# Side work of a transformer block rescheduled: weighting ahead of the feed on VectorE, evacuation ahead of the exponentials on ScalarE

## The reference, cut to what matters

```python
# block 1: mixer with two attentions, then experts
h = rms_norm(x); z = h @ w_in                   # 2848 columns and two gates of 1024
out_a = fox_attention(norm(q), norm(k), v, log_sigmoid(f + b_forget)) @ w_fox_up   # 8 heads of 64
out_b = nsa_attention(...) @ w_nsa_up           # 8 heads: window, selected and compressed keys
x = x + (sigmoid(g_a) * out_a + sigmoid(g_b) * out_b) @ w_out
x = x + moe(rms_norm(x))                        # 16 experts, 4 groups, top-2 within the top-1 group
# compressed keys and values: gelu(blocks @ w1) @ w2, once for keys and once for values
# layers 0 and 1, each
z = rms_norm(x) @ w_in_2                        # q f i z of a gated recurrence; q k v z of an attention
att = silu(za) * softmax(rope(q) rope(k) + band, with sinks) v        # 16 heads of 64, window 128
hg = recurrence(silu(q), bounded sigmoid(f), i), normed and times silu(z)
x = x + rms_norm([hg, att] @ w_out_2)
```

## Time and profile before

| | |
|---|---|
| time, median of 3 runs | 1223.36 us (1220.58 to 1223.96) |
| the profiled execution's own time | 1213.91 us |
| its span, first to last instruction | 1212.1 us |
| mean granted clock of PE | 0.945 |
| busy: PE, DVE, ACT, POOL | 1063.1, 851.1, 663.9, 44.8 us |
| memory read | 209 MB, 173 GB/s over the span |

### The profile page before, as it was taken

The page is one execution under the profiler, slowest core; times in us unless marked ns, Lnnn a source line. Parts: engine busy times, 40 slices in busy tenths (PEclk is TensorE's granted clock), DMA queues, the critical chain, the costliest instruction groups (busy, mean ns, idle before and its releaser), DMA issues.

```text
span 1212.1 us, 16479 instructions
## 1 busy us (share of the span) xinstructions
PE 1063.1 (88%) x6109; PEld 908.8 (75%) x6109; DVE 851.1 (70%) x1653; ACT 663.9 (55%) x1318; POOL 44.8 (4%) x44
## 2 busy tenths in 40 slices
PE   5798888797799999999978798799988879779997
PEld 4675866687688787878858787688777868668876
DVE  5657744574599999999857565586656755658673
ACT  5334534554588888788743657422444365642342
POOL 0201000000101000010000000000100000000010
PEclk9989989898799999999989988899999889889999
DMA  8412316133199999999933323223335322223320
GB/s 329 174 70 81 129 38 236 75 111 134 54 395 366 365 373 357 376 357 386 355 122 132 112 105 105 70 105 132 129 139 191 136 77 102 105 70 131 113 104 35
DMA packets 30035, 211.31 MB, mean 174 GB/s; under 512 B 3584, under 2 KB 3712, under 8 KB 4992
## 3 DMA queue, kind: packets, MB, share of 16 engines
q1 hardware_dynamic: 28368, 205.01, 45.5%
q10 hardware_dynamic: 1584, 5.20, 1.2%
HBM read 209.15 MB, written 1.05 MB: 173 GB/s over the span
## 4 chain that ended last, share of the span: by engine, by line
PE 48%; DVE 29%; ACT 11%; DMA 7%; issue 3%; POOL 1%; SPq 0%; DVEq 0%; POOLq 0%; ACTq 0%
PE ps L505 12%; DVE w_lo L396 11%; PE ps L507 11%; PE ps L506 11%; DMA ring<-in_panels 7%; PE ps L510 4%; PE ps L940 3%; ACT s_buf L1798 3%; ACT w_hi L1751 3%; PE ps L655 2%; DVE s_buf L399 2%; DVE s_buf L396 2%; DVE stat L1197 1%; PE ps L711 1%; DVE scr L396 1%
## 5 line engine op out<-in xcount | busy, mean ns | idle before, releaser
L396 DVE TENSOR_TENSOR w_lo<-ring,w_hi 128x512 fp32r<-128x512 f32 x760 | 482.3, 689 | 180.0 <-ACT w_hi L1751 178.9
L1751 ACT ACTIVATE w_hi<-ring 128x512 fp32r<-128x512 f32 x760 | 426.0, 620 | 206.1 <-PE ps L507 165.5
L505 PE MATMUL ps<-w_hi,op_hi 128*128 128x512 f32 (+2 forms) x800 | 317.6, 397 | 19.8 <-ACT zin L1751 4.9
L507 PE MATMUL ps<-w_hi,op_lo 128*128 128x512 f32 (+2 forms) x800 | 310.3, 388 | 0.0
L506 PE MATMUL ps<-w_lo,op_hi 128*128 128x512 f32 (+2 forms) x800 | 310.2, 388 | 0.0
L505 PEld LDWEIGHTS ps<-w_hi,op_hi 128*128 128x128 f32 x800 | 152.5, 191 | 55.2 <-DVE w_lo L396 11.9
L507 PEld LDWEIGHTS ps<-w_hi,op_lo 128*128 128x128 f32 x800 | 152.5, 191 | 31.0
L506 PEld LDWEIGHTS ps<-w_lo,op_hi 128*128 128x128 f32 x800 | 152.7, 191 | 27.3
L505 PE MATMUL ps<-op_hi,w_hi 128*128 128x256 f32 x544 | 161.1, 296 | 1.2 <-DVE op_lo L396 1.2
L506 PE MATMUL ps<-op_lo,w_hi 128*128 128x256 f32 x544 | 157.0, 289 | 0.0
L507 PE MATMUL ps<-op_hi,w_lo 128*128 128x256 f32 x544 | 156.5, 288 | 0.0
(11 more groups left out here) (245 smaller groups left out, 1135.2 us busy)
## 6 DMA issues: line engine op xcount, KB each, us to landing
ring<-in_panels SPq DMA_DIRECT2D x194, 1024.0 KB, 6.5
cst<-in_c ACTq DMA_DIRECT2D x1, 1219.0 KB, 5.3
buf_a<-in_pre ACTq DMA_DIRECT2D x2, 512.0 KB, 6.7
keys<-in_post ACTq DMA_DIRECT2D x2, 512.0 KB, 3.4
out<-x_tok SPq DMA_DIRECT2D x2, 512.0 KB, 2.6
cst<-in_c ACTq DMA_DIRECT2D x1, 960.0 KB, 6.3
x_tok<-in_x SPq DMA_DIRECT2D x1, 512.0 KB, 4.7
x_tok<-in_x ACTq DMA_DIRECT2D x1, 512.0 KB, 4.9
```

Source lines behind the costliest of these rows:

```text
L396: return V.tensor_tensor(o, a, b, op)
L505: T.matmul(o, l[0], r[0], start=start, stop=False)
L507: return T.matmul(o, l[1], r[0], start=False, stop=stop)
L1751: return A.activation(o, a, ACT.Copy, scale=scale)
```

## The change

It moves side work between takes and changes the order within a take. On DVE `ahead` runs weigh and scores_out first and the feed after them. On ACT the exponentials move from `ahead` to `behind`, so a take's evacuation stands between the copy of transposes and the exponentials. In block 1 the head sums and norms are one step each for q and k, the forget gate's inputs come at take 11, its products behind the k transposes, `lower` (bounds and router split) at take 4, nsa_gates at 12, gate_on at 39 behind the compress step. Both products of the compress MLP go into one bank side by side, with one Gelu behind the second. In the layers rope and its transposes are three steps each (q half, q half, k); the last four attention rows come one take earlier; za_on is two halves at 13 and 20; qf_on is at 29 and 33 (26 and 34 before), att_split at 37 and 39 (34 and 35 before).

```diff
@@ -85,7 +85,7 @@
-SWA_AT = (13, 15, 17, 19, 22, 24, 27, 29, 31, 33)
+SWA_AT = (13, 15, 17, 19, 22, 24, 26, 28, 30, 32)
...
@@ -153,28 +153,30 @@
 def beside_block1():
-    table = {9: [("fox_sums", 0)], 11: [("fox_norms", 0)], 12: [("fox_q", 0)], 13: [("fox_k", 0)],
-             20: [("win_sums", 0)], 21: [("win_norms", 0), ("nsa_gates", 0), ("nsa_side", 0)], 22: [("nsa_side", 1)],
-             23: [("nsa_side", 2)], 24: [("slc_sums", 0)], 25: [("slc_norms", 0)], 26: [("nsa_side", 3)],
-             38: [("gate_on", 0)], 41: [("gate_on", 1)]}
+    table = {4: [("lower", 0)], 9: [("fox_sums", 0)], 10: [("fox_sums", 1)], 11: [("fox_norms", 0), ("forget", 0)],
+             12: [("fox_norms", 1), ("fox_q", 0), ("nsa_gates", 0)], 13: [("fox_k", 0)],
+             20: [("win_sums", 0)], 21: [("win_norms", 0), ("nsa_side", 0)], 22: [("nsa_side", 1)],
+             23: [("nsa_side", 2)], 24: [("slc_sums", 0)], 25: [("slc_norms", 0)], 26: [("nsa_side", 3)]}
-    table.setdefault(43, []).append(("up_split", 0))
+    for take, name, arg in ((39, "gate_on", 0), (41, "gate_on", 1), (43, "up_split", 0)):
+        table.setdefault(take, []).append((name, arg))
 def beside_layer(l):
-    table = {b + 9: [("rope", l)], b + 11: [("swa_sides", l)]}
+    table = {b + take: [(name, (l, i))] for take, name, i in (
+        (4, "rope", 0), (6, "swa_sides", 0), (8, "rope", 1), (9, "rope", 2), (10, "swa_sides", 1), (11, "swa_sides", 2))}
-    for take, name, arg in ((18, "za_on", l), (26, "qf_on", (l, 0)), (27, "qf_bound", (l, 0)), (34, "qf_on", (l, 1)),
-                            (34, "att_split", (l, 0)), (35, "qf_bound", (l, 1)), (35, "att_split", (l, 1))):
-        table.setdefault(b + take, []).append((name, arg))
+    for take, name, i in ((13, "za_on", 0), (20, "za_on", 1), (29, "qf_on", 0), (30, "qf_bound", 0), (33, "qf_on", 1),
+                          (34, "qf_bound", 1), (37, "att_split", 0), (39, "att_split", 1)):
+        table.setdefault(b + take, []).append((name, (l, i)))
...
@@ -600,17 +602,17 @@
                 pe.wait_ge(heads_done, 1)
                 for i in range(2):
                     pair_turns(ZFQ + 2 * i * P, 2 + i, z3).then_inc(side_T, 1)
+
+            def fox_k_(_):
+                pe.wait_ge(heads_done, 2)
+                for i in range(2):
+                    pair_turns(ZFK + 2 * i * P, 4 + i, z3).then_inc(side_T, 1)
                 pe.wait_ge(ld_c1, 16)
                 pe.wait_ge(forget, 1)
                 lf2 = stat[:, 64:80]
                 T.matmul(ps[:, 6, 0:8], ntri[:, 0:P], lf2[:, 0:8], start=True, stop=True)
                 T.matmul(ps[:, 6, 8:16], ntri[:, P:2 * P], lf2[:, 0:8], start=True, stop=False)
                 T.matmul(ps[:, 6, 8:16], ntri[:, 0:P], lf2[:, 8:16], start=False, stop=True).then_inc(side_T, 1)
-
-            def fox_k_(_):
-                pe.wait_ge(heads_done, 2)
-                for i in range(2):
-                    pair_turns(ZFK + 2 * i * P, 4 + i, z3).then_inc(side_T, 1)
 
             def nsa_side(n):
                 c, kind = SIDES[n]
...
@@ -701,17 +703,15 @@
-                    if step == 4:
-                        pe.wait_ge(cmp_a, 1)
-                            m = T.matmul(ps[0:64, 7, 0:256], blk[c][:, 8 * h + n, :, :].rearrange("p g n -> p (g n)"),
+                            m = T.matmul(ps[0:64, 7, c * 256:(c + 1) * 256], blk[c][:, 8 * h + n, :, :].rearrange("p g n -> p (g n)"),
-                    pe.wait_ge(cmp_a, 2)
+                    pe.wait_ge(cmp_a, 1)
...
@@ -1093,10 +1095,10 @@
-            def fox_sums(_):
+            def fox_sums(n):
-                head_sums(HEADS_FOX)
+                head_sums(HEADS_FOX[n:n + 1])
             def win_sums(_):
...
@@ -1118,21 +1120,26 @@
+            def fox_q(_):
+                lf, lx, la = stat[:, 64:80], stat[:, 80:96], stat[:, 96:112]
+                dve.wait_ge(forget_l, 1)
+                dv(ts(lx, lx, 0.0, None, ALU.min))
+                settle()
+                tt(lf, lx, la, ALU.subtract).then_inc(forget, 1)
-                dve.wait_ge(forget_l, 1)
-                dv(ts(lx, lx, 0.0, None, ALU.min))
-                settle()
-                tt(lf, lx, la, ALU.subtract).then_inc(forget, 1)
-                dve.wait_ge(side_T, 3)
-                ts(stat[:, 112:128], ps[:, 6, 0:16], -1.0, None, ALU.mult).then_inc(side, 1)
             def fox_k_(_):
-                    dve.wait_ge(side_T, 4 + i)
+                    dve.wait_ge(side_T, 3 + i)
+                dve.wait_ge(side_T, 5)
+                ts(stat[:, 112:128], ps[:, 6, 0:16], -1.0, None, ALU.mult).then_inc(side, 1)
+            def lower(_):
...
@@ -1249,7 +1256,7 @@
-                dve.wait_ge(za_on, l + 1)
+                dve.wait_ge(za_on, 2 * l + r // 4 + 1)
...
@@ -1487,37 +1494,41 @@
-            def rope(l):
...
+            def rope(arg):
+                l, i = arg
+                c, n, dst = ((ZQA, 8, tm(scr)[:, :, 0:512]), (ZQA + 512, 8, tm(scr)[:, :, 512:1024]),
+                             (ZKA, 2, tm(pt_buf[:, 1024:1280])))[i]
+                m = TT * n * half
+                    dve.wait_ge(out_free[a], OUT_L1 + OUT_L2 * l + 1 + i)
+                dve.wait_ge(pre_T, 4 * l + 4)
+                dve.wait_ge(roped, 3 * l + i)
+                v = zb3[:, :, c:c + n * HD].rearrange("p a (h d) -> p a h d", h=n)
+                d4 = dst.rearrange("p a (h d) -> p a h d", h=n)
+                u1, u2 = (y[:, 0:m].rearrange("p (a h d) -> p a h d", a=TT, h=n) for y in (s_buf, pt_buf))
...
+            def swa_sides(arg):
+                l, i = arg
...
...
@@ -1655,10 +1667,10 @@
                      "head_scale": head_scale}
 
             def ahead(t):
-                feed(2 * t + AHEAD)
                 for name, arg in beside.get(t, ()):
                     if name in ("weigh", "scores_out"):
                         table[name](arg)
+                feed(2 * t + AHEAD)
...
@@ -1812,10 +1825,12 @@
-            def silu_za(l):
+            def silu_za(arg):
+                l, i = arg
-                    act.wait_ge(out_free[b], OUT_L1 + OUT_L2 * l + 5)
-                A.activation(za, za, ACT.Silu).then_inc(za_on, 1)
+                    act.wait_ge(out_free[b], OUT_L1 + OUT_L2 * l + 4 + i)
+                o = za[:, i * 1024:(i + 1) * 1024]
+                A.activation(o, o, ACT.Silu).then_inc(za_on, 1)
             def qf_on(arg):
...
@@ -1846,12 +1861,10 @@
             def compress(step):
-                if step in (3, 4):
-                    c = step - 3
+                if step == 4:
-                    A.activation(scr[0:64, c * 256:(c + 1) * 256], ps[0:64, 7, 0:256],
-                                 ACT.Gelu_apprx_tanh).then_inc(cmp_a, 1)
+                    A.activation(scr[0:64, 0:512], ps[0:64, 7, :], ACT.Gelu_apprx_tanh).then_inc(cmp_a, 1)
...
@@ -1990,12 +2003,12 @@
             def ahead(t):
-                    if name in ("turn_out", "scores_out"):
+                    if name == "turn_out":
             def behind(t):
-                    if name in table and name not in ("turn_out", "scores_out"):
+                    if name in table and name != "turn_out":
...
@@ -2063,7 +2076,7 @@
-                        act.wait_ge(swa_T, 5 * l + 5)
+                        act.wait_ge(swa_T, 5 * l + 4)
...
```

More of the change, by code:

```diff
@@ L738, in compress @@
                     pe.wait_ge(cmp_f, 1)
-                    pe.wait_ge(cmp_a, 3 + a)
+                    pe.wait_ge(cmp_a, 2 + a)
                     for r in range(PAIRS):
@@ L744, in compress @@
                     a = step - 11
-                    pe.wait_ge(cmp_a, 5)
+                    pe.wait_ge(cmp_a, 4)
                     if a == 1:
@@ L911, in combine @@
                                 m.then_inc(back_mm, 1)
[L913 to L916, removed]
+            def swa_sides(arg):
+                l, i = arg
+                pe.wait_ge(roped, 3 * l + i + 1)
+                if i < 2:
+                    for a in range(TT):
                         for n in range(4):
@@ L920, in swa_sides @@
                         m.then_inc(swa_T, 1)
+                    return
                 for a in range(TT):
@@ L1110, in slc_sums, with forget_in @@
                 head_sums(HEADS_SLC)
-            def fox_q(_):
-                lf, lx, la = (stat[:, c:c + 16].rearrange("p (a h) -> p a h", a=TT) for c in (64, 80, 96))
+            def forget_in(_):
+                lx, la = (stat[:, c:c + 16].rearrange("p (a h) -> p a h", a=TT) for c in (80, 96))
                 for a in range(TT):
@@ L1180, in scores_out @@
                 if job < FOX_JOBS:
-                    dve.wait_ge(side, 3)
+                    dve.wait_ge(side, 5)
                     for a, lo, n in ((1, 0, S), (0, S, P)):
@@ L1324, in compress @@
                     tt(sc3, sc3, bc(mx, CMP_PAD), ALU.subtract).then_inc(cmp_s, 1)
-                    dve.wait_ge(cmp_a, 3)
+                    dve.wait_ge(cmp_a, 2)
                     dv(V.tensor_reduce(sm, sc3, AX, ALU.add))
```

(51 more changed lines are left out.)

2 lines of the change are left out of this document (1 added, 1 removed).

## The result

| | before | after |
|---|---|---|
| time, median of 4 runs | 1221.97 us (1211.00 to 1223.96) | 1151.15 us (1143.45 to 1152.56) |
| ratio, 95% interval | 1 | 0.9425 (0.9354 to 0.9495) |
| the profiled execution's own time | 1213.91 us | 1152.56 us |
| its span | 1212.1 us | 1150.7 us |
| mean granted clock of PE | 0.945 | 0.962 |

A forecast was written before the change was run, and what follows sets the result against it. PE, 88% busy, waits for small results queued behind unneeded work on ACT and DVE. Terms 23.5 + 27.4 + 10 = 61 us off 1213.9 give 1153, median 1162; range 1142 to 1182, whole range 1138 to 1192.

The forecast's parts named there:

- The basic cycle: Each attention job: weighted scores ready 5.8 us after its scores end instead of 8.0, wanted at 6.6; such waits vanish.
- the terms for qf_on and job 7: Layers: moving qf_on from take 26 gains 5.2 plus 1.2 us; a new wait of 3.6 before job 7's values.
- Exponentials behind the evacuation: Block 1, takes 15 and 19: waits fall to 0.45 us each, gain 4.0; layers: cost 0.1 each.
- take 24: In each layer: wait 1.49 becomes 1.3 us, since the reload of Exp follows the evacuation; gain 0.2.
- The forget gate: Block 1, takes 12 and 13: its matmul's wait of 4.57 us becomes about 0.7; gain 3.9.
- Gelu: Block 1: one Gelu for both halves ends ACT's 13.1 us wait and PE's 0.59 and 3.78; gain 4.4 us.
- Takes 11, 31, 39 and the window norms: Block 1 waits: take 11 3.35 to 3.9 us, 31 3.79 to 2.9, 39 7.34 to 2.7, norms 1.11 to 2.3.
- Rope: Each layer: split in halves, its wait of 3.67 us becomes 2.1 in all; gain 1.6.
- Job 0: Each layer: za_on's Silu and table loads delay the exponentials to 5.2 us; wait 3.30 becomes 1.9, gain 1.4.
- Job 7 and level 0: Each layer: new wait 3.6 us before job 7's values; level 0's 7.17 becomes 3.4 plus 0.7 for level 1.
- The drain at a table switch: Skill's 1.38 us drain beside each table load would make it 8 us worse in all; the forecast went by the rows.
- The clock: PE regains time run below full clock after waits: 33 us in all, bounds 0 to 25, 10 taken.

The follow-up runs named there:

- the last two kernels: Changed kernel with qf_bound, q's Silu, head sums, norms, DVE copies and rope moved: 1124.85 us; that one with exponentials ahead of the evacuation in the layers: 1120.12 us.
- the kernels of 1139 and 1202 us: Changed kernel with first-half qf_bound at take 32 and q's second Silu at 31: 1138.74 us; changed kernel with DVE's feed first again: 1202.04 us.
- three such steps: On the changed kernel, cumulatively: qf_bound and q's Silu moved, 1138.74 us; head sums, norms, copies and rope moved, 1124.85; exponentials ahead of evacuation in layers, 1120.12.
- the best kernel: Changed kernel with all three leftover steps, the last putting exponentials ahead of the evacuation in the layers only: 1120.12 us, ratio 0.9187.

## Why the prediction was right, and where its terms were off

**The basic cycle.** The count of 5.8 us with the weighting first, against 6.6 wanted, held: in block 1 the first five waits became one of 0.64 (and one of 0.26 where none was), and DVE's order turned out to carry more than half of the change. What the count did not say is that this edit and the rest need each other. Every term was reckoned with the order already in place. For a sum of the whole change that is right, for the worth of a part it is not: of the 11.3 us of waits that belong to neither part, 5.6 and 5.7 a layer, some 4 in each lie at the last three jobs, inside the terms for qf_on and job 7, and 1.6 at takes 22 and 24.

**Exponentials behind the evacuation.** Block 1: two waits of 0.47 and 0.43 for 0.45 each. Layers: 0.1 each was the forecast, 0.31 at takes 26 to 30 and 0.50 at take 22 came (this one not by ACT's order, it stays when that is undone), and take 24 has 1.73 for 1.3. Reckoned as a gain of 4.0 - 0.8, it is a zero, as its undoing shows.

**The forget gate.** 0.7 was kept, none shows: its matmul at 60.26 us follows the transposes at once.

**Gelu.** The term of 4.4 was measured in its place, since both waits are gone, but given to the wrong edit: two Gelus cost 1.43 in one wait and nothing that shows in the time. That the sum holds there is luck. ACT's 13.1 us in front of the Gelu are not gone either: it still waits 5.99 for the second product.

**Takes 11, 31, 39 and the window norms.** 3.64 for 3.9, 2.50 for 2.9, 2.66 for 2.7, 2.31 for 2.3.

**Rope.** 0.64 + 1.52 = 2.16 for 2.1. With the second half at take 9 and its transposes at 11, as the last two kernels have it, the 1.52 is gone and nothing came in its place.

**Job 0.** 0.82 for 1.9, the largest miss. I counted a table load in front of the Silu at take 13. There is none:

```profile
638.55 0.60 ACT L1763 ACTIVATE scr<-ps 128x512 f32<-128x512 f32 x1 [1.72 <-PE ps L509]
639.24 1.06 ACT L1833 ACTIVATE scr<-scr 128x1024 f32<-128x1024 f32 x1
640.21 1.14 ACT L1763 ACTIVATE w_hi<-ring 128x512 fp32r<-128x512 f32 x2
641.36 1.28 ACT L1811 ACT_TABLE_LOAD   x1
642.65 0.51 ACT L1811 ACTIVATE s_buf<-s_buf,stat 128x256 f32<-128x256 f32 x1
```

Nothing had used another table since the last Silu, that of the experts, and the copies in between (w_hi and the evacuations) have no load before them. The exponentials start 4.1 us after the copy's start, not 5.2: the load of 1.28 that isn't there makes up the miss. In the kernel before the exponentials stood between, so its trace had that load and I carried it over.

**Job 7 and level 0.** The new wait of 3.6 came as 3.67; level 0 has 3.67 for 3.4, and level 1 none for 0.7.

**The drain at a table switch.** The Trainium skill, "ScalarE: Activation LUTs", What ACT_TABLE_LOAD costs, has about 1.38 us of drain beside the load. The trace doesn't agree; as an estimate, with that page's drain job 0's wait would have been 0.82 + 1.38 = 2.2 or more. In the rows above the instruction before the load ends at its start (640.21 + 1.14 = 641.35), and the next ACTIVATE starts 642.65 - 641.36 = 1.29 us after it. In all eleven kernels it is 1.29 or 1.30 wherever that ACTIVATE waits for no other engine, so going by the rows was right.

**The clock.** 9.9 for 10, but made up otherwise than I reckoned. The stretches at under full clock add up to some 133 us of the span before and 86 after. Those of block 1 fell from 34 to 10 us, those of the two layers from 71 to 41: there PE's busy time fell by 6.3 and by 2.1 + 6.3, more than the 10 in all. But in the routing, which the change doesn't touch, two of 6.8 and 17.1 us became one of 30.7, which took 3.1 back, and the experts' stage took 1.4. That the sum is 9.9 all the same is luck. Before (293 to 317 us) and after (262 to 293):

```profile
293.00:317.00 24.00, 15.34 (x80) 14.70 (x81) 15.02 (x65) 8.35 (x16) 0.00 (x0) 0.57 0.01 3
```

```profile
262.00:293.00 31.00, 21.14 (x86) 19.92 (x87) 16.12 (x66) 9.79 (x18) 0.18 (x1) 0.50 0.01 3
```

From the first transposes there (after a wait of 6.18 in both) to the products of L805, 21.1 us became 24.2. Four of the nine experiments had the long stretch, among them the kernels of 1139 and 1202 us. The other five took 20.6 to 20.8 us. What decides between the two is open; nothing tried here separates it. With the short one the clock term would have been about 13.

## What to carry to other kernels

- Where one queue makes weights ahead and also serves the engine that sets the end, put first what that engine waits for next, and the feed after it, as long as the buffers cover the delay: here one moved line gave 37.6 us. Check that by counting from one event on the bound engine to what is ready and what is wanted.
- Such an order and the places of long side work have to be judged together: 20 + 37.6 us apart were 70.8 together, and 10.6 + 29.7 us of waits were 51.6.
- The best order can differ by stage, depending on whether the next take's bank is wanted before the small result; and each leftover wait, read back to what stands in front of it, was worth another step (31 us for three such steps; by the profiled executions about half of it waits, half PE's clock).

## What the runs showed of the hardware

- A wait's length alone doesn't say whether the clock falls. In the kernel after, the wait of 2.50 us at 150.79 left it at full; the same wait, 2.48 at 149.94, in the kernel with the attention rows moved back, whose block 1 is the same, is followed by a low stretch. The one of 1.73 at 684.99 has one too, and so have 2.66 at 204.52 and 3.67 at 723.15. Stretches of windows (busy times, then PEclk), first that kernel, then the kernel after:

```profile
150.00:158.00 8.00, 8.00 (x36) 5.11 (x37) 6.17 (x16) 3.24 (x10) 0.00 (x0) 0.79 0.26 71
...
150.00:158.00 8.00, 7.21 (x40) 4.91 (x41) 6.83 (x20) 3.21 (x10) 0.00 (x0) 1.00 0.22 85
684.00:692.00 8.00, 7.01 (x46) 6.28 (x47) 6.04 (x15) 3.02 (x7) 0.00 (x0) 0.79 0.37 133
723.00:731.00 8.00, 7.85 (x44) 6.77 (x45) 2.74 (x6) 2.34 (x3) 0.00 (x0) 0.79 0.37 133
```

  0.79 is a mean of the two levels, 1.2 and 2.4 GHz. In the kernel before, a wait of 3.67 us in layer 0 left PE at full clock, and its twin in layer 1 did not; the same sixteen transposes behind it took 1.97 and 3.67 us:

```profile
657.25 1.97 PE L510 MATMUL ps<-ident,scr 128*128 128x128 f32 x16 [3.67 <-DVE scr L396]
...
953.18 3.67 PE L510 MATMUL ps<-ident,scr 128*128 128x128 f32 x16 [3.68 <-DVE scr L396]
```

  "TensorE: Matmul & The Clock Gate", HAM oscillation, of the Trainium skill tells of a matmul loop whose waits of about 3 to 5 us each throttle PE, so that each burst then starts cold. In the kernel after, the eight waits of 3.10 to 6.18 us behind the first agree; the 3.67 at 657.25 does not, and waits of 1.73 and 2.66 were followed by low stretches too, so by these traces it is no rule for a single wait.
- The same routing stage took 21.1 or 24.2 us in kernels that differ only elsewhere; PE's busy time in it was 12.9 and 16.0 us at the same 74 products, so the 3.1 between them are the granted clock (0.58 and 0.50).
- The time that the clock gives back is a good part of what removed waits bring: from before to the best kernel the span fell by 95.8 us, 26.8 of them in PE's busy time at the same 6109 instructions.
